# A hybrid decoder layer with a planned instruction order: expert rows ranked over all other steps, retention and the sample's logits as streams of their own

## The chip, the cores and the metric

The kernel runs on one core of one Trainium2 chip. The metric is device time in microseconds of one execution; the median of three runs before the change is 3858.67 us (3858.39 to 3861.91). The profile is of one further execution, which took 3870.04 us with a span of 3868.2 us from the first to the last instruction.

## The reference

One inference step of one decoder layer, for a prompt of 1024 tokens and a sample of 8 sequences with 4 new tokens each (32 tokens) over a paged cache of 2048 past tokens. All data are 32-bit floats.

```
xn  = rms_norm(x);  one projection of 1024 to 3400 columns gives q,k,v / indexer q,k,weights / retention q,k,v,gate
att = for every query: indexer score of every earlier key, keep the best 256, softmax attention over those (8 heads of 64)
ret = chunkwise retention (4 heads of 128, chunk 128, a state carried from chunk to chunk), group norm, swish gate
h   = x + concat(att, ret) @ w_out
n   = rms_norm(h);  8 heads: q = n @ w_q, two sets of 128 sub-keys, top 16 of each, top 16 of the 256 sums -> 128 experts per token
y   = h + sum over the 128 experts e of  gate_e * gelu(n . u[e]) * v[e]        # u, v: 16384 rows of 1024
out = rms_norm(y); also k, v, indexer k and the retention states
```

The expert part dominates the traffic: for each of 128 tokens of a tile and each of 128 expert slots the kernel reads one row of u and the row of v beside it (2048 floats, 8 KB).

## The kernel before

The 1024 prompt tokens are 8 tiles of 128 (t = 0 to 7); the 32 sample tokens are a ninth tile, SAMPLE (t = 8). First all nine tiles go through the input projection (step `project`), to about 470 us. Everything after that comes in one list of steps, `schedule`, which `make_schedule` (L342) writes before the kernel is built. Each engine walks that list and issues its own part of every step, so the list is the program order of each of the five in-order queues; semaphores alone hold the engines together. A step that waits holds up everything behind it on its engine.

Per tile there are three kinds of work.

- The front (`front_steps`, L226): load the projected rows into Hb, transpose q and k (`turn`), score all earlier keys (`score` on TensorE and ScalarE, `scored` on VectorE), the retention (`decay`, `decayed`, `hold`, `carry`, `carried`, `retained`), the search for the best 256 keys (`topk`: 32 rounds of MAX8 and MATCH_REPLACE8 on VectorE, L1345 and L1346), the mask, attention (`attend`, `soften`), `mixed`, and the transposes of the mix (`mixT`). The sample's front has its own steps: indexer keys gathered from the cache by sequence (`sscores`), retention with eight states (`sdecay`, `sret`, `skd`, `sstate`, `sstated`, `sstored`), its `topk` over 2080 keys on 32 partitions, then K and V gathered by sequence and attention in two groups of four sequences (`slogits`, `smask`, `sexp`, `sprobs`, `svalue`, `sout`). In the list the sample's `slogits` of sequences 0 to 3 stand between rounds of `topk`, in fixed places.
- The back (`back_steps`, L288): `out` (w_out in eight chunks, streamed in by SyncE), `norm`, queries, sub-key scores, the two levels of top 16 (`top`, `cand`, `best`), and `pick`, whose last instruction (L1467) says that the tile's experts are chosen.
- The expert stream: 128 rows per partition for a tile, 32 for the sample (where four partitions' worth of slots are packed). GpSimd gathers row after row (L1838, 128 x 8 KB each) into a ring of 8. Rows go in pairs (`unit`). VectorE multiplies and sums each u row with the normed tokens (the dot, L1484), ScalarE takes Gelu (L1755), VectorE multiplies by the gate (the coefficient, L1475), ScalarE writes a diagonal matrix of the coefficient (L1747), and TensorE adds diag x v into `yacc` (`sums`, L1030). Only then is the ring's slot free for the gather 8 rows later. `seed` (L1020) starts yacc with the residual, `ycopy` (L1763) copies it out, `finish` norms and stores it.

The coefficient of pair k-1 is no step: it stands inside `unit` k, behind the first of its two dots (L1485, `if k and s == PAIR * k: weigh_pair(t, k - 1)`); ScalarE's part of `unit` k writes the diagonals of pair k-1 first and then waits for pair k's dots. The last pair of a tile has a step `drain`.

The planner keeps two clocks, one for TensorE and one for VectorE, and takes at each turn the step that can start first; among those that can start within NEAR (0.4 us) of it, the one with the earliest due time. A front's steps are due evenly over PERIOD = 400 us from (t - 2) * PERIOD - 150 us, a back's over 360 us from (t - 1) * PERIOD, and dots and sums have due times as well:

```
yield "D", at, t * PERIOD + PERIOD * k / units(0), "unit"
yield "P", weighed[t, k] + 1.0, t * PERIOD + PERIOD * k / units(0), "sums"
```

So a front step that is due earlier than a pair comes before that pair. Fronts go one after another, so do backs; a back begins when its tile's front is done, the tile before is seeded and the tile two before is finished. `ycopy` follows the last sums of its tile in the list at once. It writes `ykeep`, which shares its place with nT, the next tile's transposed norm.

Of the kernel before, what the change touches and what calls it, by code (L numbers as in the profile page):

```python
# [226 lines left out]
def front_steps(t):  # L227
# [4 lines left out]
    if t < TILES:  # L232
# [10 lines left out]
        steps += [Step("decay", t, 0, "P", 1.2), Step("decayed", t, 0, "D", 2.3, 1, 0.3), Step("hold", t, 0, "P", 2.4, 1, 0.5),  # L243
                  Step("carry", t, 0, "P", 1.2, 0, 0.5), Step("carried", t, 0, "D", 1.4, 1, 0.3),
                  Step("retained", t, 0, "D", 2.3), Step("retained", t, 1, "D", 2.2), Step("retained", t, 2, "D", 2.6)]
# [9 lines left out]
    else:  # L255
        steps = [Step("load", t, 0, "", 0, 1, 12.0), Step("sheads", t, 0, "P", 3.0, 1, 2.5), Step("spad", t, 0, "D", 4.0, 2, 0.3),
                 Step("sdecay", t, 0, "P", 1.2, 2), Step("sdecayed", t, 0, "D", 4.5, 1, 0.3), Step("sret", t, 0, "P", 10.0, 1, 0.5)]
        for k in range(NB + 1):
            if k < NB:
                steps += [Step("skd", t, k, "D", 0.6, 0, 0.3), Step("sstate", t, k, "P", 1.7, 1, 0.4)]  # L260
            if k:
                steps += [Step("sstated", t, k - 1, "D", 1.4, 3 if k == 1 else 4 if k < NB else 2, 0.3)]
        steps += [Step("sstored", t, 0, "D", 0.2, 0, 0.3)]
        steps += [Step("retained", t, 0, "D", 2.3), Step("retained", t, 1, "D", 2.2), Step("retained", t, 2, "D", 2.6)]
        steps += [Step("sturn", t, 0, "P", 2.3), Step("sspread", t, 0, "D", 2.6, 1, 0.3), Step("swi", t, 0, "P", 2.8, 1, 0.4),
# [20 lines left out]
    return steps + [Step("mixT", t, 0, "P", 2.6, 1, 2.4)]  # L286


def back_steps(t):
# [15 lines left out]
    return steps  # L305

# [35 lines left out]
PERIOD, LEAD, ROW, LATENCY, NEAR = 400.0, 150.0, 2.62, 3.4, 0.4  # L342


def make_schedule():
# [11 lines left out]
    fronts = [Stream(front_steps(t), (t - 2) * PERIOD - LEAD, PERIOD) for t in range(TILES + 1)]  # L357
    backs = [Stream(back_steps(t), (t - 1) * PERIOD, 0.9 * PERIOD) for t in range(TILES + 1)]
    front = back = 0
    rows_at = 0.0  # L360
    chosen, keyed, mixed, seeded, finished, kept = {}, {}, {}, {}, {}, {}
    dotted, weighed, summed = {}, {}, {}
    dot, pair, drained = (0, 0), (0, 0), 0
# [9 lines left out]
    def heads():  # L373
        if front <= TILES:
            yield "front", fronts[front]
        if back <= TILES:
            yield "back", backs[back]

    def candidates():
        for kind, stream in heads():  # L380
            e = stream.head()
            what, t, _ = e.entry
            ready = stream.ready()
            names = (claimed + claims(*e.entry))[max(len(claimed) - 4, 0):]
            if any(freed_later(name) not in listed and freed_later(name) for name in names[:-4]):
                continue
            if what == "mixT" and t:
# [20 lines left out]
        if t in seeded and (t, k) in weighed:  # L408
            yield "P", weighed[t, k] + 1.0, t * PERIOD + PERIOD * k / units(0), "sums"
# [4 lines left out]
    while len(finished) <= TILES:  # L414
# [10 lines left out]
        if kind in ("front", "back"):  # L425
            stream = fronts[front] if kind == "front" else backs[back]
# [11 lines left out]
            if what == "mixT":  # L438
                mixed[t] = end
            if stream.head() is None and kind == "front":  # L440
                front += 1
            elif stream.head() is None:
                chosen[t] = end
                back += 1
        elif kind == "unit":
# [1495 lines left out]
```

## Time and profile before

| what | value |
|---|---|
| median of three runs | 3858.67 us |
| the profiled execution, its span | 3870.04 us, 3868.2 us |
| TensorE, VectorE, ScalarE, GpSimd busy | 82%, 69%, 26%, 32% of the span |
| TensorE's mean granted clock | 0.930 of full |
| read from and written to HBM | 1220.50 MB, 22.46 MB |
| gathers of expert rows | 1056 of 1.05 MB |

The stretches that count are read from tables of windows: busy time of each engine, the granted clock, the share of time in which the 16 DMA engines were busy, and the rate in GB/s. The rate is the one to watch in the expert stream, since each gather moves the same 1.05 MB.

### The profile page before, as it was taken

The numbers are of one execution on the slowest core, as the hardware profiler recorded it, in microseconds if no ns is written. First come the engines' busy times: TensorE is split into PE (matmuls) and PEld (weight loads), VectorE is DVE, ScalarE is ACT, GpSimd is POOL, SyncE is SP. The second block draws the span as 40 slices with busy tenths as digits, with TensorE's granted clock in tenths as the row PEclk, the third lists the DMA queues.
The fourth block names the chain that finished last, engine by engine and source line by source line (L and its number), as shares of the span: only waits on it lengthen the run. The fifth ranks groups of instructions, "written<-read, shape, count | busy, mean of one in ns | idle before, by whom it ended". The sixth has DMA issues, their size and how long they took to land.

```text
span 3868.2 us, 31404 instructions
## 1 busy us (share of the span) xinstructions
PE 3178.7 (82%) x9551; PEld 1543.8 (40%) x9551; DVE 2674.1 (69%) x6543; ACT 993.7 (26%) x2512; POOL 1237.8 (32%) x1084
## 2 busy tenths in 40 slices
PE   5999864988798879887987898689887389879776
PEld 2444253443354325433543453245433144334321
DVE  1222138888868778978888888988856998434655
ACT  1111122152134214421432153115222022311211
POOL 0000001444444434443443344234342124333443
PEclk9999977999999999998999899899999699889999
DMA  4111133999999999999999999889998179988998
GB/s 170 57 66 50 54 116 134 391 417 397 392 404 407 415 370 369 394 399 361 397 400 368 364 385 408 341 341 384 356 394 340 70 297 420 392 338 343 414 421 341
DMA packets 190425, 1245.72 MB, mean 322 GB/s; under 512 B 22704, under 2 KB 27184, under 8 KB 50672
## 3 DMA queue, kind: packets, MB, share of 16 engines
q0 software_dynamic: 155520, 1128.34, 72.4%
q1 hardware_dynamic: 34736, 115.37, 7.9%
q8 instruction: 77, 1.26, 0.1%
q14 instruction: 92, 0.75, 0.1%
HBM read 1220.50 MB, written 22.46 MB: 321 GB/s over the span
## 4 chain that ended last, share of the span: by engine, by line
PE 44%; DMA 26%; DVE 24%; issue 3%; ACT 1%; SPq 1%; POOL 1%; DVEq 0%; ACTq 0%; POOLq 0%
PE yacc L1030 23%; DMA weights<-in_uv,eid 19%; PE bank L857 11%; DVE weights L1484 7%; DVE kv L1346 3%; DVE tiny L1345 3%; PE bank L993 3%; DMA weights<-in_w_out 2%; PE bank L967 2%; DVE weights L1416 1%; DVE weights L1215 1%; DVE weights L1412 1%; DMA kv<-in_cache_ik,gi 1%; POOL weights L1838 1%; ACT diag L1747 1%
## 5 line engine op out<-in xcount | busy, mean ns | idle before, releaser
L1030 PE MATMUL yacc<-weights,diag 128*128 128x512 f32 (+1 forms) x4224 | 2002.5, 624 | 364.7 <-ACT diag L1747 363.4
L1838 POOL DMA_INDIRECT weights<-in_uv,eid x1056 | 1210.5, 1146 | 2578.1 <-PE yacc L1030 1875.8
L1484 DVE CUSTOM_DVE_ANT_0 weights<-weights,xn 128x1024 f32<-128x1024 f32 x1056 | 1290.2, 1224 | 597.5 <-DMA weights<-in_uv,eid 585.8
L1030 PEld LDWEIGHTS yacc<-weights,diag 128*128 128x128 f32 (+1 forms) x4224 | 802.5, 196 | 1453.6 <-issue 909.3
L1747 ACT ACTIVATE diag<-main,coef 128x128 f32<-128x128 f32 x1024 | 356.7, 394 | 1450.8 <-DVE coef L1475 1381.1
L1345 DVE MAX8 tiny<-kv 128x8 f32<-128x384 f32 (+6 forms) x224 | 245.0, 1094 | 3.0
L1755 ACT ACTIVATE gl<-hv 128x2 f32<-128x2 f32 x528 | 107.1, 203 | 530.6 <-DVE hv L1484 529.9
L1346 DVE MATCH_REPLACE8 kv<-tiny,kv 128x384 f32<-128x384 f32 (+6 forms) x224 | 241.6, 1079 | 0.0
L967 PE MATMUL bank<-weights 128*128 128x512 f32 (+1 forms) x288 | 158.4, 687 | 87.0 <-DMA weights<-in_w_out 85.8
L857 PE MATMUL bank<-weights 128*128 128x512 f32 (+3 forms) x560 | 229.6, 572 | 0.0
L857 PE MATMUL bank<-weights,mid 128*128 128x512 f32 (+1 forms) x448 | 183.2, 570 | 0.0
L857 PEld LDWEIGHTS bank<-weights 128*128 128x128 f32 (+1 forms) x560 | 97.4, 175 | 130.2 <-issue 125.4
L993 PEld LDWEIGHTS bank<-weights 128*128 128x128 f32 x1152 | 133.9, 192 | 16.0 <-issue 15.6
L1250 DVE TENSOR_TENSOR weights<-Hb,weights 128x80 f32<-128x80 f32 (+5 forms) x15 | 5.8, 387 | 190.6 <-ACT tinya L1637 190.3
L993 PE MATMUL bank<-weights 128*128 128x128 f32 (+1 forms) x1152 | 134.1, 275 | 0.8 <-ACT weights L1708 0.8
L967 PEld LDWEIGHTS bank<-weights 128*128 128x128 f32 (+1 forms) x288 | 56.7, 206 | 175.9 <-issue 173.9
L1416 DVE FIND_INDEX8 weights<-weights 128x8 uint32<-128x128 f32 (+1 forms) x396 | 125.4, 328 | 0.0
L857 PEld LDWEIGHTS bank<-weights,mid 128*128 128x128 f32 x448 | 84.8, 190 | 96.7 <-issue 91.8
L1412 DVE MAX8 weights<-weights 128x8 f32<-128x128 f32 (+1 forms) x396 | 112.6, 325 | 3.0 <-ACT weights L1732 1.6
L1250 DVE TENSOR_TENSOR weights<-spare,weights 128x80 f32<-128x80 f32 (+2 forms) x12 | 4.7, 389 | 142.2 <-ACT tinya L1637 141.9
L1475 DVE TENSOR_TENSOR coef<-gl,gate 128x2 f32<-128x2 f32 x528 | 82.3, 156 | 15.0 <-ACT gl L1755 14.6
L921 PEld LDWEIGHTS bank<-kv,mid 128*128 128x128 f32 x576 | 75.6, 198 | 35.0 <-issue 20.9
(240 smaller groups left out, 2309.8 us busy)
## 6 DMA issues: line engine op xcount, KB each, us to landing
weights<-in_w_out SPq DMA_DIRECT2D x72, 512.0 KB, 7.8
weights<-in_uv,eid POOLq DMA_INDIRECT x1056, 9.8
Hb<-h_scratch SPq DMA_DIRECT2D x8, 1700.0 KB, 10.7
weights<-in_w_in SPq DMA_DIRECT2D x6, 2048.0 KB, 18.8
h_scratch<-Hb SPq DMA_DIRECT2D x4, 1700.0 KB, 5.5
h_scratch<-spare SPq DMA_DIRECT2D x4, 1700.0 KB, 5.5
nw<-in_wffn SPq DMA_DIRECT2D x9, 512.0 KB, 6.4
nw<-in_wfin SPq DMA_DIRECT2D x9, 512.0 KB, 14.3
```

The lines of the kernel that those rows point to most:

```text
L857: mm = nc.tensor.matmul(b[0:R, 0:w], xT[t % 2][:, k, 0:R], win[:, k, 512 * n:512 * n + w], start=(k == 0), stop=(k == KC - 1))
L967: mm = nc.tensor.matmul(b[0:R, :], mixT[:, k, 0:R], wout_sb[i % 2][:, 512 * (k - k2):512 * (k - k2 + 1)], start=(k == 0), stop=(k == KC - 1))
L993: mm = nc.tensor.matmul(b[:, (h % 4) * R:(h % 4 + 1) * R], wq_sb[:, k, h * P:(h + 1) * P], nT[:, k, 0:R], start=(k == 0), stop=(k == KC - 1))
L1030: mm = nc.tensor.matmul(yacc[0:W, 512 * j:512 * (j + 1)], diag[:, n % 4, 0:W], ring[:, n % RING, D + 512 * j:D + 512 * (j + 1)], start=Fal ...
L1345: link(V.max(tiny[0:R, 40:48], a))
L1346: link(V.match_replace(a, tiny[0:R, 40:48], a, CHOSEN))
L1412: ins = V.max(vals[:, half], a)
L1416: ins = V.max_index(idxs[:, half], vals[:, half], a)
L1484: ins = V.tensor_tensor_reduce(u, u, xn[:, t % 2, :], 1.0, 0.0, ALU.mult, ALU.add, hv[:, n % RING:n % RING + 1])
L1747: A.activation(diag[:, n % 4, 0:W], select[:, 0:W], ACT.Copy, scale=coef[:, n % RING:n % RING + 1]).then_inc(diag_ready, 1)
L1755: A.activation(gl[:, c:c + PAIR], hv[:, c:c + PAIR], ACT.Gelu).then_inc(gelu_ready, 1)
L1838: pool.indirect_dma_start(dst, None, table, bass.IndirectOffsetOnAxis(ap=ids, axis=0)).then_inc(s, 16)
```

## The change

All of it but a few lines lies in the planner; no arithmetic is changed.

- `drain` is gone and the coefficient is a step `weigh` of its own on VectorE, with ScalarE's diagonals as its part there. It may start 0.75 us behind the pair's dots in the planner's clock.
- `unit`, `weigh` and `sums` have constant due times far below every other step's, so that among steps which can start within NEAR of the first they always come first. NEAR is 0.1 instead of 0.4.
- The retention of each tile leaves the front and becomes a stream (`side_steps`) that may begin when the tile's q and k are transposed. `attend` part 3, `mixT` and the sample's first `sscores` wait in the plan for its end; the sample's `sturn` waits for `sret`.
- The sample's `slogits` of sequences 0 to 3 leave the fixed places between `topk` rounds and become a stream (`past_steps`) that may begin when the sample's scores are in place; `smask` waits for its end. GpSimd's first K gather gets a wait for the sample's gated retention (`gated`). The sample's Silu moves from `retained` part 0 to part 1.
- `ycopy` becomes an entry of its own that waits in the plan for the next tile's `keys`.
- PERIOD is 360 instead of 400, LEAD 100 instead of 150; the sample's front is due 200 us later than the rule for the others gives, and over 0.8 of a period.

```diff
-PERIOD, LEAD, ROW, LATENCY, NEAR = 400.0, 150.0, 2.62, 3.4, 0.4
+PERIOD, LEAD, AHEAD, LATER, LAST, ROW, LATENCY, NEAR = 360.0, 100.0, 0.0, 200.0, 0.8, 2.62, 3.4, 0.1
@@ front_steps
-        steps += [Step("decay", t, 0, "P", 1.2), ... Step("retained", t, 2, "D", 2.6)]
@@ the sample's front
-        for k in range(ROUNDS):
-            steps += [Step("topk", t, k, "D", 4.8, 0, 0.3)]
-            if k % 8 in (1, 2, 3, 4, 5, 6):
-                steps += [Step("slogits", t, (k // 8, k % 8 - 1), "P", 2.0, 2)]
+        steps += [Step("topk", t, k, "D", 4.8, 0, 0.3) for k in range(ROUNDS)]
+def past_steps():
+    return [Step("slogits", SAMPLE, (b, c), "P", 2.0, 1, 1.2 if c < 5 else 4.0) for b in range(4) for c in range(6)]
@@ make_schedule
+    sides = [Stream(side_steps(t), (t - 2) * PERIOD - LEAD, 0.5 * PERIOD) for t in range(TILES + 1)]
+    pasts = [Stream(past_steps(), (SAMPLE - 2) * PERIOD + LATER, PERIOD)]
@@ candidates
+            if what == "mixT" or (what, part) in (("attend", 3), ("sscores", 0)):
+                if t not in held:
+                    continue
+                ready = max(ready, held[t])
-        if t in chosen and drained == t:
+        if due:
+            yield "D", dotted[due[0]] + 0.75, -2e7, "weigh"
+        if t in chosen:
-                yield "D", at, t * PERIOD + PERIOD * k / units(0), "unit"
-        if drained < t:
-            yield "D", dotted[drained, units(drained) - 1] + 0.8, -1e9, "drain"
+                yield "D", at, -1e7, "unit"
-            yield "P", weighed[t, k] + 1.0, t * PERIOD + PERIOD * k / units(0), "sums"
+            yield "P", weighed[t, k], -1e7, "sums"
+        if copying and (copying[0][0] == TILES or copying[0][0] + 1 in keyed):
+            yield "", copying[0][1], 0.0, "ycopy"
@@ VectorE
-                    if k and s == PAIR * k:
-                        weigh_pair(t, k - 1)
@@ ScalarE
-                if k:
-                    spread_pair(t, k - 1)
@@ GpSimd, slogits of sequence 0
+                    pool.wait_ge(gated, TILES + 1)
```

## Rows read from the trace of the kernel before

**Rows 1.** The page's first line.

```profile
span 3868.2 us, 31404 instructions
```

**Rows 2.** Windows of the expert streams (tiles 0-5, 6, 7, sample, quiet): stretch, length, busy (x), clock, DMA, GB/s.

```profile
650.00:2898.00 2248.00, 1920.50 (x5843) 953.39 (x5841) 1864.42 (x4578) 684.07 (x1677) 915.97 (x782) 0.94 0.96 385
2898.00:3417.00 519.00, 391.23 (x1268) 186.24 (x1264) 388.98 (x719) 122.23 (x307) 154.01 (x146) 0.88 0.77 308
3417.00:3778.00 361.00, 282.51 (x745) 122.07 (x744) 180.57 (x406) 62.71 (x204) 140.40 (x128) 0.93 0.95 382
3778.00:3868.20 90.20, 62.13 (x132) 13.98 (x130) 47.70 (x114) 12.65 (x49) 26.81 (x24) 0.93 0.82 336
3625.00:3775.00 150.00, 113.50 (x245) 44.47 (x244) 76.10 (x151) 26.91 (x90) 64.93 (x61) 0.99 1.01 421
```

**Rows 3.** Timeline of VectorE, the sample's key search: start, length, line, operation, tiles.

```profile
2964.68 2.32 DVE L1345 MAX8 tiny<-kv 32x8 f32<-32x2080 f32 x1
...
2967.11 2.30 DVE L1346 MATCH_REPLACE8 kv<-tiny,kv 32x2080 f32<-32x2080 f32 x1
...
3055.82 1.22 DVE L1484 CUSTOM_DVE_ANT_0 weights<-weights,xn 128x1024 f32<-128x1024 f32 x1
```

**Rows 4.** Timeline of TensorE there; in brackets the idle time before, and what ended it.

```profile
3057.62 6.43 PE L1030 MATMUL yacc<-weights,diag 128*128 128x512 f32 x8 [78.51 <-ACT diag L1747]
```

**Rows 5.** Waits in 650:2898 of TensorE, in 650:2732 of VectorE: total, times, longest.

```profile
PE bank L967 <- DMA weights<-in_w_out: 63.7, 12, 14.6
...
DVE weights L1484 <- DMA weights<-in_uv,eid: 246.7, 227, 9.5
```

**Rows 6.** Timeline of VectorE in the quiet stretch: two dots and a coefficient.

```profile
3644.71 1.23 DVE L1484 CUSTOM_DVE_ANT_0 weights<-weights,xn 128x1024 f32<-128x1024 f32 x1 [1.17 <-DMA weights<-in_uv,eid]
...
3647.19 1.23 DVE L1484 CUSTOM_DVE_ANT_0 weights<-weights,xn 128x1024 f32<-128x1024 f32 x1 [1.24 <-DMA weights<-in_uv,eid]
...
3648.34 0.16 DVE L1475 TENSOR_TENSOR coef<-gl,gate 128x2 f32<-128x2 f32 x1
```

**Rows 7.** Timeline of VectorE, retention of tile 0: first and last instruction.

```profile
488.05 0.69 DVE L1307 TENSOR_TENSOR spare<-bank,dec 128x512 f32<-128x512 f32 x1 [17.32 <-PE bank L879]
...
502.06 0.69 DVE L1301 TENSOR_TENSOR Hb<-Hb 128x512 f32<-128x512 f32 x1
```

**Rows 8.** Windows up to the end of the sample's search, and behind it (columns as Rows 2).

```profile
650.00:2732.00 2082.00, 1782.02 (x5368) 886.74 (x5366) 1758.07 (x4342) 644.82 (x1567) 846.58 (x726) 0.95 0.96 386
2732.00:2964.70 232.70, 200.97 (x663) 94.25 (x663) 136.94 (x308) 53.67 (x150) 89.60 (x75) 0.93 0.96 381
2964.70:3152.00 187.30, 92.02 (x344) 46.86 (x344) 184.41 (x177) 33.80 (x80) 32.13 (x32) 0.76 0.45 171
3152.00:3277.00 125.00, 113.05 (x365) 54.56 (x366) 105.69 (x323) 34.20 (x86) 48.13 (x45) 0.93 0.93 375
```

**Rows 9.** Window 2898:3152, the dots alone (two instructions each): VectorE, clock, DMA, GB/s.

```profile
2898.00:3152.00 254.00, 51.45 (x84) 0.83 0.60 232
```

**Rows 10.** Timelines: end of tile 7's front, end of search, sample's experts chosen, its seed.

```profile
2731.57 0.69 DVE L1382 TENSOR_TENSOR Hb<-bank,tiny 128x512 f32<-128x512 f32 x1
3151.99 1.23 DVE L1356 TENSOR_SCALAR kv<-kv 32x2080 f32<-32x2080 f32 x1
3612.93 0.19 DVE L1467 TENSOR_TENSOR gate<-gate,tiny 128x32 f32<-128x32 f32 x1
3777.68 1.95 PE L1020 MATMUL yacc<-h,main 32*128 32x512 f32 x4 [1.27 <-ACT weights L1764]
```

**Rows 11.** The page's DMA issues: KB, median us from issue to landing.

```profile
weights<-in_uv,eid POOLq DMA_INDIRECT x1056, 9.8
```

**Rows 12.** ScalarE: groups of loads ahead of Gelu (count, busy, mean ns), then timeline.

```profile
L1755 ACT ACT_TABLE_LOAD x65 | 83.4, 1283 | 1.2
...
2244.34 1.28 ACT L1755 ACT_TABLE_LOAD   x1
2245.64 0.20 ACT L1755 ACTIVATE gl<-hv 128x2 f32<-128x2 f32 x1
```

More of the change, by code:

```diff
@@ L256, in front_steps @@
         steps = [Step("load", t, 0, "", 0, 1, 12.0), Step("sheads", t, 0, "P", 3.0, 1, 2.5), Step("spad", t, 0, "D", 4.0, 2, 0.3),
[L257 to L260, printed above, removed]
-            if k:
[L262 to L265, printed above, removed]
+                 Step("sturn", t, 0, "P", 2.3, 1), Step("sspread", t, 0, "D", 2.6, 1, 0.3), Step("swi", t, 0, "P", 2.8, 1, 0.4),
                   Step("swiT", t, 0, "D", 1.6, 1, 0.3)]
@@ L356, in make_schedule @@
     clock = {"P": 0.0, "D": 0.0}
-    fronts = [Stream(front_steps(t), (t - 2) * PERIOD - LEAD, PERIOD) for t in range(TILES + 1)]
-    backs = [Stream(back_steps(t), (t - 1) * PERIOD, 0.9 * PERIOD) for t in range(TILES + 1)]
-    front = back = 0
+    fronts = [Stream(front_steps(t), (t - 2) * PERIOD - LEAD + (t == SAMPLE) * LATER, PERIOD if t < TILES else LAST * PERIOD)
+              for t in range(TILES + 1)]
+    backs = [Stream(back_steps(t), (t - 1) * PERIOD - AHEAD, 0.9 * PERIOD) for t in range(TILES + 1)]
+    sides = [Stream(side_steps(t), (t - 2) * PERIOD - LEAD, 0.5 * PERIOD) for t in range(TILES + 1)]
+    pasts = [Stream(past_steps(), (SAMPLE - 2) * PERIOD + LATER, PERIOD)]
+    front = side = back = past = 0
     rows_at = 0.0
     chosen, keyed, mixed, seeded, finished, kept = {}, {}, {}, {}, {}, {}
-    dotted, weighed, summed = {}, {}, {}
-    dot, pair, drained = (0, 0), (0, 0), 0
+    turned, held, returned, placed = {}, {}, [], []
+    dotted, weighed, summed, copying = {}, {}, {}, []
+    dot, due, pair = (0, 0), [], (0, 0)
     def arrival(t, k):
@@ L375, in heads @@
             yield "front", fronts[front]
+        if side <= TILES and side in turned:
+            yield "side", sides[side]
+        if not past and placed and SAMPLE in held:
+            yield "past", pasts[past]
         if back <= TILES:
@@ L381, in candidates @@
             e = stream.head()
-            what, t, _ = e.entry
+            what, t, part = e.entry
             ready = stream.ready()
@@ L386, in candidates @@
                 continue
+            if what in ("decay", "sdecay"):
+                ready = max(ready, turned[t])
+            if what == "mixT" or (what, part) in (("attend", 3), ("sscores", 0)):
+                if t not in held:
+                    continue
+                ready = max(ready, held[t])
+            if what == "sturn":
+                if not returned:
+                    continue
+                ready = max(ready, returned[0])
+            if what == "slogits" and part == (0, 0):
+                ready = max(ready, held[t], placed[0])
+            if what == "smask" and part == (0, 0):
+                if not past:
+                    continue
+                ready = max(ready, pasts[0].ends[-1])
             if what == "mixT" and t:
@@ L424, in make_schedule @@
             start = max(clock[on], start)
-        if kind in ("front", "back"):
-            stream = fronts[front] if kind == "front" else backs[back]
+        if kind in ("front", "side", "back", "past"):
+            stream = {"front": fronts[front:], "side": sides[side:], "back": backs[back:], "past": pasts}[kind][0]
             e = stream.head()
@@ L439, in make_schedule @@
                 mixed[t] = end
+            if (what, part) in (("turn", 3), ("spad", 0)):
+                turned[t] = end
+            if what == "sret":
+                returned.append(end)
+            if what == "splace":
+                placed.append(end)
+            if what == "retained" and part == 2:
+                held[t] = end
             if stream.head() is None and kind == "front":
                 front += 1
+            elif stream.head() is None and kind == "side":
+                side += 1
+            elif stream.head() is None and kind == "past":
+                past += 1
             elif stream.head() is None:
@@ L1755, in unit @@
                 A.activation(gl[:, c:c + PAIR], hv[:, c:c + PAIR], ACT.Gelu).then_inc(gelu_ready, 1)
-            def drain(t, part):
-                spread_pair(t, units(t) - 1)
             def ycopy(t, part):
```

51 lines of the change are left out of this document (30 added, 21 removed).

## The prediction

> **What bounds the kernel now.** I read the windows of the expert streams first. In the quiet stretch nothing but pairs of rows is left, and there the DMA engines are busy all the time at 421 GB/s [rows 2]. A row is 1.05 MB, so a row every 2.49 us is the ceiling, and time below it can be counted as lost: length times (1 - rate/421). Tiles 0 to 5 lose 2248 x (1 - 385/421) = 192 us, tile 6 loses 519 x (1 - 308/421) = 139 us, tile 7 loses 361 x (1 - 382/421) = 33 us. That is 364 us out of 3128. VectorE and TensorE are not far behind the DMA: in 650 to 2732 they are busy 84% and 86% [rows 8]. So three resources are nearly full, and the order decides how well they overlap.
>
> Next I read where tile 6 loses its time. VectorE starts the sample's search at 2964.68 and takes the next dot at 3055.82; between them lie 19 rounds of 4.76 us (a MAX8 of 2.32, a replace of 2.30, a short load) and one small addition [rows 3]. TensorE stands 78.5 us, waiting for a diagonal [rows 4]. The rows in the ring had long landed: the plan had put the search, due earlier, in front of the dots. The window of the search runs at 171 GB/s and loses 187.3 x (1 - 171/421) = 111 us by itself [rows 8].
>
> Last I read what the end hangs on. The sample's experts are chosen at 3612.9, its seed comes only at 3777.7, when tile 7 is done [rows 10]. The sample was 165 us early, the stream was late. Then 90.2 us follow to the end [rows 2].
>
> **The change part by part.** No instruction goes except the coefficient's place; the arithmetic is the same, so everything is a matter of waits.
>
> *Dots and sums first.* The search stall goes. A round of search can now stand before a pair only if the pair was not there when the round began, 4.76 us at most, against 8 rows x 2.49 = 19.9 us in the ring. The gain is at least the 78.5 us of TensorE's wait and at most all 139 us that tile 6 loses. Tile 7, which has no search beside it, still loses 33 us, so I take 100.
>
> *The coefficient as its own step.* In the quiet stretch a pair's second dot ends at 3645.94 and its coefficient starts at 3648.34, behind the next pair's first dot [rows 6]: 2.4 us, of which Gelu needs 0.20 [rows 12]. So about 2.2 us of a slot's 19.9 come back. Where the DMA runs at the ceiling that is worth nothing; where slots run out it is worth up to that. This and the rank work on the same 192 us of tiles 0 to 5. Of these, 63.7 us of TensorE waiting for chunks of w_out [rows 5] are not touched: SyncE still issues `finish`, `resid` and the w_out loads in that order. Between nothing and 192 - 64 = 128 us can come back; VectorE and TensorE, both over 84% busy, have no room for all. I take half, 64 us, a third of the 192.
>
> *Retention as a stream.* On tile 0 the retention stands on VectorE from 488.05 to 502.75 ahead of the mask, and VectorE had been idle 17.3 us before it [rows 7]. Run beside attention it saves 0 to 14.7 us ahead of the first chosen tile; I take 7. For the later tiles it is work for VectorE's gaps and counted below. What is late in its place is attention itself, which shares TensorE's banks.
>
> *Logits, gather wait, ycopy.* The 24 sample logits ran between search rounds and now run beside them. An estimate of one step per pair in the quiet stretch, 24 x 2 x 2.49 = 120 us, is covered by the search's 32 x 4.76 = 152 us, so `smask` waits for the search as before: nothing. The wait on GpSimd has row gathers queued behind it, so every microsecond of it would stop the stream; it ends with the retention, which the plan puts before the scores: nothing. `ycopy` behind the next tile's keys costs nothing as long as those are early, and the sample's experts were 165 us early [rows 10]; with that cover gone, seed and all sums of the next tile wait behind it on TensorE.
>
> *The sum for the streams.* 100 + 64 + 7 = 171 us. Tile 7 ends at 3778 - 171 = 3607.
>
> *The price: the sample comes later.* Dots before the search means the search ends later, and the sample was not far enough ahead for the whole of it. Up to the end of the search at 3152 VectorE idles (2082 - 1758) + (232.7 - 136.9) + (187.3 - 184.4) = 423 us [rows 8, 10]. By then tile 6 had 84/2 = 42 dots [rows 9]. In the new order tile 6 is nearly through when the search ends, some 120 dots: 78 more at 51.45/42 = 1.23 us and half a coefficient of 0.16 [rows 6], 1.31 us together: 102 us. Tile 7's back has to be done by then too; before, VectorE did most of it in 3152 to 3277, where it was busy 105.7 us, of which 125 us x 375 GB/s = 45 rows account for 59 us [rows 8]: 47 us more. Against this stands idle time won back. In 650 to 2732 VectorE waits 246.7 us for rows in 227 places [rows 5], with other work in the list behind the wait; with the coefficient free and the retention as filler I take a third of the 324 us, as for the streams: 108 us. Bounds are nothing and the 247 us. The search then ends at 3152 + 102 + 47 - 108 - 7 = 3186. From there to the sample's experts it took 3613 - 3152 = 461 us, through logits, V gathers, w_out and the back, on engines shared with a stream as now: chosen at 3647. That is 40 us after tile 7 has ended. The first row lands 9.8 us later [rows 11], then 90.2 us: 3747.
>
> The span falls from 3868.2 [rows 1] by 121 us. The profiled execution took 3870.04 us, 11.4 above the median of the runs, so against the median: 3858.7 - 121, about 3740.
>
> **The rivals.**
>
> *The streams set the end* (0.20). If VectorE wins back more than 160 us of its 423, the sample is chosen before tile 7 ends, and the end is 3607 + 90 = 3697, against the median 3688, down to 3640 if the streams win back all that w_out leaves. For it: 0.96 of the DMA's time is busy in 650 to 2898 already [rows 2], so little is missing. Against it: VectorE's load in the late tiles.
>
> *The plan's clocks don't hold* (0.17). The order is fixed before the run; if the planned arrivals miss, VectorE still stands before a dot with other work behind it, as in those 227 places. Then only the search stall and the 7 us go (85 us), VectorE wins nothing back, fewer rows are done by then (some 100: 76 us), and the search ends at 3152 + 76 + 47 - 7 = 3268: chosen at 3729, end at 3829, against the median 3820.
>
> *Slower: VectorE waits in the coefficient, and the sample's search is pushed past the end of the streams* (0.18). The coefficient now follows its own dots and not the next pair's first dot, so the time Gelu needs is no longer covered. Gelu is often late: 65 times a table load of 1.28 us stands before it [rows 12], usually because an Exp of the attention came between. If nothing is planned in that gap, VectorE, with all front and back steps queued behind, stands up to 65 x 1.28 = 83 us. For it: those loads lie in the attention, where VectorE has no slack. Against it: the plan puts the coefficient 0.75 us behind the dots and takes any other ready step in between. With nothing won back and 83 us lost the search ends at 3294 + 83 = 3377, the experts are chosen at 3838; the last stretch then runs without a stream beside it, which I put at 45 us shorter, and the end is 3893, against the median about 3880. It decides from a loss of about 13 us: with 13 us more idle than before the search ends at 3307, and 3307 + 461 + 100 is the old end.
> The Trainium skill (ScalarE: Activation LUTs, What ACT_TABLE_LOAD costs) states about 1.28 us for the load and 1.38 us of drain, 2.66 us for every switch. By that the 65 loads would make 173 us and this rival some 90 us worse. The trace agrees with the load and shows no drain behind it: the load at 2244.34 ends at 2245.62 and Gelu starts at 2245.64 [rows 12], so the sum goes by 1.28.
>
> **How the numbers follow.** My forecast has 0.45, its own range is 3690 to 3800. The range over all cases is 3640 to 3880: below lies the best of the first rival, above half of the slower one. 0.2%, some 8 us, is about what a measurement of this kernel can tell from no change. Forecast, first and second rival make 0.82; of the second's upper edge 0.04 falls within 0.2%, and of the slower one's lower edge 0.03. So faster 0.78, the same 0.07, slower 0.15.
>
> **What would show it.** Right: no search round stands in front of landed rows for more than two rounds, and TensorE's longest wait for a diagonal is under 20 us; in the quiet stretch the coefficient starts within 1 us of its dots; the window from the first to the last tile reaches over 395 GB/s in tiles 0 to 5; the sample's experts are chosen after tile 7's last sums, and the DMA rate has a hole of some 50 us between. The waits for w_out stay near 64 us. Wrong: coefficients that wait for Gelu more than 60 us in total; a search that ends before 3100 or after 3300; a tile other than the sample whose experts come after the tile before has ended; a gather on GpSimd that waits for the retention.

## The result, and the profile after

The changed kernel takes 3920.53 us (median; 3914.46 to 3922.50) against 3860.29 for the one before on the same chip: a ratio of 1.0153 [1.0135, 1.0170], 1.5% slower. The forecast of 3740 us was wrong in sign and outside its range. The profiled execution has a span of 3920.6 us, 52.4 longer than [rows 1].

First the page: the span, and the rate in 40 slices of 98 us. Two slices stand out: the 34th (3234 to 3332) with 11 GB/s and the 39th (3725 to 3823) with 95.

```profile
span 3920.6 us, 31491 instructions
...
GB/s 168 67 61 42 80 88 184 394 411 411 378 400 400 421 367 394 414 380 366 420 414 373 381 410 412 420 399 405 289 265 411 410 366 11 249 421 405 385 95 345
```

The kernel before has one such slice, the 32nd with 70 GB/s, which lies in its search; its page:

```profile
GB/s 170 57 66 50 54 116 134 391 417 397 392 404 407 415 370 369 394 399 361 397 400 368 364 385 408 341 341 384 356 394 340 70 297 420 392 338 343 414 421 341
```

Next the windows, with the columns of [rows 2]: up to the end of tile 7's front, up to the start of the sample's search, the search, up to the choice of the sample's experts, and the rest. The sixth is the first empty stretch, the part of the search that runs alone; the last is the second.

```profile
650.00:2805.30 2155.30, 1857.59 (x5564) 921.66 (x5564) 1831.68 (x4477) 658.39 (x1646) 882.24 (x767) 0.96 0.97 395
2805.30:3164.00 358.70, 283.30 (x945) 141.45 (x945) 216.47 (x607) 74.21 (x209) 127.81 (x119) 0.89 0.90 364
3164.00:3349.00 185.00, 74.66 (x198) 29.78 (x198) 179.01 (x155) 30.95 (x76) 25.35 (x23) 0.72 0.35 139
3349.00:3818.00 469.00, 369.89 (x1142) 180.17 (x1142) 214.47 (x468) 95.13 (x260) 152.40 (x139) 0.88 0.79 323
3818.00:3920.00 102.00, 60.80 (x128) 13.20 (x128) 52.22 (x118) 12.84 (x50) 32.93 (x32) 0.90 0.84 341
3237.00:3341.00 104.00, 14.20 (x51) 5.45 (x50) 102.53 (x67) 11.30 (x21) 0.94 (x1) 0.58 0.03 10
3775.00:3817.00 42.00, 29.01 (x129) 24.89 (x128) 14.55 (x62) 4.92 (x8) 0.00 (x0) 0.50 0.00 2
```

The first row answers to the first of [rows 8]: up to the end of tile 7's front the rate rose from 386 to 395 GB/s, but that front ended 74 us later (2805 against 2732). VectorE's idle time there is 2155.3 - 1831.7 = 324 us; before it was 2082 - 1758 = 324 us. Up to that point of the work not a microsecond came back.

The waits of the whole execution say where rows stopped (total, times, longest). GpSimd's wait for a choice of experts contains 647.3 us ahead of tile 0, which the kernel before has too; what is left is 240.4 us in three places, and before there was none.

```profile
POOL weights L1875 <- DVE gate L1514: 887.7, 4, 647.3
DVE weights L1531 <- DMA weights<-in_uv,eid: 484.8, 407, 10.4
...
PE yacc L1077 <- ACT diag L1789: 282.6, 194, 22.3
...
PE bank L1014 <- DMA weights<-in_w_out: 120.3, 17, 31.4
...
PE bank L1210 <- DVE kv L1403: 98.1, 1, 98.1
DVE coef L1522 <- ACT gl L1795: 91.0, 122, 14.4
```

The timelines show the three places. First GpSimd, with the idle time in brackets: the gather that starts tile 6, tile 7 and the sample each waits for its choice.

```profile
2812.34 0.94 POOL L1875 DMA_INDIRECT weights<-in_uv,eid  x1 [30.98 <-DVE gate L1514]
...
3369.44 0.94 POOL L1875 DMA_INDIRECT weights<-in_uv,eid  x1 [125.29 <-DVE gate L1514]
...
3818.07 0.94 POOL L1875 DMA_INDIRECT weights<-in_uv,eid  x1 [84.14 <-DVE gate L1514]
```

Then ScalarE, copying out tile 6:

```profile
3242.54 0.60 ACT L1800 ACTIVATE weights<-yacc 128x512 f32<-128x512 f32 x1 [2.65 <-PE yacc L1077]
```

Tile 6 ended at 3243, 165 us earlier than before (3408), and tile 7's experts were not yet chosen. TensorE:

```profile
3350.10 7.21 PE L1210 MATMUL bank<-kv,dec 32*128 32x512 f32 x8 [98.15 <-DVE kv L1403]
```

It stands 98 us in the sample's masked attention (`smask`), waiting for the end of the search. VectorE shows why both wait:

```profile
3232.22 2.31 DVE L1392 MAX8 tiny<-kv 32x8 f32<-32x2080 f32 x1
...
3339.40 2.30 DVE L1393 MATCH_REPLACE8 kv<-tiny,kv 32x2080 f32<-32x2080 f32 x1
3341.73 2.29 DVE L1262 TENSOR_TENSOR weights<-weights,main 128x2048 f32<-128x2048 f32 x1
...
3348.82 1.23 DVE L1403 TENSOR_SCALAR kv<-kv 32x2080 f32<-32x2080 f32 x1
...
3368.88 0.29 DVE L1514 TENSOR_TENSOR gate<-gate,tiny 128x128 f32<-128x128 f32 x1
...
3817.61 0.19 DVE L1514 TENSOR_TENSOR gate<-gate,tiny 128x32 f32<-128x32 f32 x1
```

From 3237 to 3342 stand 22 search rounds without a break (MAX8 and replace, 2.3 us each), behind the last coefficient of tile 6; only then come the last steps of tile 7's choice (the TENSOR_TENSOR of 3341.73 is the first), done at 3368.88. The sample is chosen at 3817.61.

VectorE again, a coefficient in the quiet stretch:

```profile
3639.94 0.08 DVE L1531 DVE_READ_ACCUMULATOR2_ANT hv<- 128x1 f32 x1
3640.29 0.18 DVE L1522 TENSOR_TENSOR coef<-gl,gate 128x2 f32<-128x2 f32 x1 [0.27 <-ACT gl L1795]
```

It follows its dot by 0.3 us, where it stood 2.4 us behind [rows 6].

The table orders the events (us of the span; a tile is done with its last sums; "busy, idle" is VectorE's from 650 to the search's end, "rowless" GpSimd's wait for choices after tile 0's). Tile 7's copy out is no measure of its end: it now waits in the plan for the sample's keys and comes 49 us behind the last sums in the changed kernel.

| kernel | tile 6 done | tile 7 chosen | search ends | sample chosen | tile 7 done | VectorE busy, idle | rowless | ratio to before |
|---|---|---|---|---|---|---|---|---|
| before | 3408 | 3277 | 3152 | 3613 | 3776 | 2079, 423 | 0 | 1 |
| after | 3243 | 3369 | 3349 | 3818 | 3753 | 2227, 472 | 240 | 1.0153 |
| coefficient alone | 3377 | 3293 | 3144 | 3639 | 3755 | 2083, 411 | 0 | 0.9961 |
| rank alone | 3256 | 3422 | 3361 | 3816 | 3809 | 2187, 524 | 143 | 1.0151 |
| streams alone | 3372 | 3317 | 3281 | 3737 | 3786 | 2187, 444 | 0 | 1.0038 |
| all but the rank | 3337 | 3298 | 3261 | 3728 | 3762 | 2198, 413 | 0 | 0.9979 |
| all but the coefficient | 3231 | 3336 | 3316 | 3777 | 3721 | 2216, 450 | 202 | 1.0046 |
| search due 100 us later | 3234 | 3134 | 3517 | 3751 | 3583 | 2372, 495 | 132 | 0.9971 |
| rank in the search only | 3226 | 3104 | 3425 | 3725 | 3586 | 2334, 441 | 101 | 0.9908 |

### The profile page after: what moved, and what is told of

It reads as the page before. It is cut to its first block, busy times and chain, and to the rows that moved or that the text cites. A ratio compares the mean times of both kernels' runs of the same rounds, so it can differ in the third digit from the quotient of the medians.

```text
span 3920.6 us, 31491 instructions
## 1 busy us (share of the span) xinstructions
PE 3170.2 (81%) x9551; PEld 1555.6 (40%) x9551; DVE 2684.7 (68%) x6543; ACT 982.2 (25%) x2513; POOL 1222.9 (31%) x1084
## 4 chain that ended last, share of the span: by engine, by line
PE 49%; DMA 26%; DVE 17%; issue 3%; ACT 2%; POOL 2%; SPq 1%; ACTq 0%; DVEq 0%; POOLq 0%
PE yacc L1077 26%; DMA weights<-in_uv,eid 19%; PE bank L904 10%; DVE weights L1531 4%; PE bank L1040 4%; DVE kv L1393 3%; DVE tiny L1392 3%; PE bank L1014 2%; DMA weights<-in_w_out 2%; POOL weights L1875 2%; DMA out_y_p<-nw 1%; ACT diag L1789 1%; DVE weights L1262 1%; DVE weights L1463 1%; PE bank L953 1%
## 5 line engine op out<-in xcount | busy, mean ns | idle before, releaser
L1077 PE MATMUL yacc<-weights,diag 128*128 128x512 f32 (+1 forms) x4224 | 1969.9, 616 | 284.0 <-ACT diag L1789 282.6
L1875 POOL DMA_INDIRECT weights<-in_uv,eid x1056 | 1196.5, 1133 | 2630.2 <-PE yacc L1077 1681.5
L1531 DVE CUSTOM_DVE_ANT_0 weights<-weights,xn 128x1024 f32<-128x1024 f32 x1056 | 1273.0, 1223 | 491.8 <-DMA weights<-in_uv,eid 484.8
L1077 PEld LDWEIGHTS yacc<-weights,diag 128*128 128x128 f32 (+1 forms) x4224 | 792.8, 194 | 1362.3 <-issue 896.2
L1014 PE MATMUL bank<-weights 128*128 128x512 f32 (+1 forms) x288 | 156.0, 680 | 122.8 <-DMA weights<-in_w_out 120.3
L1040 PE MATMUL bank<-weights 128*128 128x128 f32 (+1 forms) x1152 | 156.9, 301 | 10.0 <-ACT weights L1750 10.0
L1040 PEld LDWEIGHTS bank<-weights 128*128 128x128 f32 x1152 | 155.4, 219 | 21.9 <-issue 12.7
L1210 PE MATMUL bank<-kv,dec 32*128 32x512 f32 x16 | 14.6, 1052 | 98.1 <-DVE kv L1403 98.1
```

The source lines that it names most:

```text
L1014: mm = nc.tensor.matmul(b[0:R, :], mixT[:, k, 0:R], wout_sb[i % 2][:, 512 * (k - k2):512 * (k - k2 + 1)], start=(k == 0), stop=(k == KC - 1))
L1040: mm = nc.tensor.matmul(b[:, (h % 4) * R:(h % 4 + 1) * R], wq_sb[:, k, h * P:(h + 1) * P], nT[:, k, 0:R], start=(k == 0), stop=(k == KC - 1))
L1077: mm = nc.tensor.matmul(yacc[0:W, 512 * j:512 * (j + 1)], diag[:, n % 4, 0:W], ring[:, n % RING, D + 512 * j:D + 512 * (j + 1)], start=Fal ...
L1531: ins = V.tensor_tensor_reduce(u, u, xn[:, t % 2, :], 1.0, 0.0, ALU.mult, ALU.add, hv[:, n % RING:n % RING + 1])
L1875: pool.indirect_dma_start(dst, None, table, bass.IndirectOffsetOnAxis(ap=ids, axis=0)).then_inc(s, 16)
```

## The experiments

Three theories stood at the start. R: the rank puts rows ahead of the sample's search, the sample becomes late, and the end is the search's end + 469 + 103 us. W: the waits for Gelu in the new coefficient step take VectorE's time. H: the 125 us hole ahead of tile 7 is the loss. After the first four kernels a fourth was formed, P: what chooses experts (fronts and backs) and what uses them (rows) share VectorE; ranking the rows first brings rows earlier and the choices later, until rows wait for a choice. The edits are excerpts; a line of `...` stands for lines left out. The experiments ran on three chips, each beside the kernel before, and the ratios are to that; a difference in us between two kernels is of their medians.

**The coefficient step alone**, put on the kernel before.

```diff
+        if due:
+            yield "D", dotted[due[0]] + 0.75, -2e7, "weigh"
...
-                    if k and s == PAIR * k:
-                        weigh_pair(t, k - 1)
```

> The kernel before with one part of the change: the coefficient is a step of its own; ranks, streams and constants are as before. Theory R (the rank of dots and sums over all other steps makes tile 7's front and the sample's search late, and the end is the search's end + 469 + 103 us): without the rank the early coefficient only helps, time 3760 to 3840, search end at 3152 or earlier. Theory W (VectorE now waits for Gelu in front of the coefficient, 91 us against 15, and that is the loss): slower than before, about 3935. Theory H (the 125 us in which nothing is gathered, since tile 7's last back steps stand behind 21 search rounds, is the loss): says nothing of this run; it would follow the place of tile 7's back.

Median 3850.27, ratio 0.9961 [0.9945, 0.9976]: faster, though 10 us above what R had expected, with nearly the waits of after. From the list of waits:

```profile
DVE weights L1482 <- DMA weights<-in_uv,eid: 468.2, 387, 5.6
...
DVE coef L1473 <- ACT gl L1746: 88.1, 141, 14.3
```

88.1 us of waiting for Gelu and a faster kernel: W falls. VectorE waits 468.2 us for rows, where before it was 585.8 in the whole execution, and 14.6 for Gelu: 600 us of both before, 556 here. Most of what it no longer waits ahead of a dot it waits ahead of a coefficient.

**All but the coefficient step**: the changed kernel with the coefficient back inside `unit`.

```diff
-        if due:
-            yield "D", dotted[due[0]] + 0.75, -2e7, "weigh"
-        if t in chosen:
+        if t in chosen and drained == t:
...
```

> The changed kernel with the coefficient put back behind the next pair's first dot (and the drain step); rank, streams and constants as changed. Theory W: VectorE's waits for Gelu fall from 91 to about 15 us and the time to about 3845. Theory R: the rank is still there, the search ends as late or later, 3350 to 3410, time 3920 to 3980. Theory H: the hole stays, time within 20 us of 3920.

3882.28, ratio 1.0046 [1.0018, 1.0075]: still slower than before, and 38 us under the changed kernel. No theory had this time: W expected 3845, H at least 3900, R at least 3920.

From its waits, in the order GpSimd, TensorE, VectorE:

```profile
POOL weights L1887 <- DVE gate L1516: 848.5, 3, 646.5
...
PE bank L1212 <- DVE kv L1405: 81.0, 1, 81.0
...
DVE coef L1524 <- ACT gl L1804: 7.1, 5, 5.2
```

The waits for Gelu are gone (7.1 us), the holes (848.5 - 646.5 = 202 us) and TensorE's stand in `smask` (81 us) are not. So the pattern belongs to the rank, and under the rank the coefficient step adds to it.

**All but the rank**: due times for dots and sums again.

```diff
-                yield "D", at, -1e7, "unit"
+                yield "D", at, t * PERIOD + PERIOD * k / units(0), "unit"
...
-            yield "P", weighed[t, k], -1e7, "sums"
+            yield "P", weighed[t, k], t * PERIOD + PERIOD * k / units(0), "sums"
```

> The changed kernel with dots and sums ranked by due time as before; coefficient step, streams and constants as changed. Theory R: tile 7's front is done before 2760 instead of 2805, the search ends 60 to 100 us earlier (3250 to 3290), time 3780 to 3860. Theory W: the coefficient step is still there, time 3900 to 3940. Theory H: if the hole stays at 100 us or more, time 3900 or more; a shorter time with the hole still there would speak against it.

3853.62, ratio 0.9979 [0.9964, 0.9994]. Taking the rank out gives 67 us back.

From its waits:

```profile
POOL weights L1875 <- DVE gate L1514: 646.9, 1, 646.9
...
DVE coef L1522 <- ACT gl L1795: 98.9, 125, 15.1
```

No hole is left (646.9 us is tile 0's), and there are more waits for Gelu than in after, 98.9 us. That is what R expected, and once more against W; for H it decides nothing, since the hole went with the rank.

**The search due 100 us later**, rank kept.

```diff
-PERIOD, LEAD, AHEAD, LATER, LAST, ... = 360.0, 100.0, 0.0, 200.0, 0.8, ...
+PERIOD, LEAD, AHEAD, LATER, LAST, ... = 360.0, 100.0, 0.0, 300.0, 0.8, ...
```

> The changed kernel with one constant: the sample's front is due 300 us late instead of 200, so that in the list all of tile 7's back stands ahead of the sample's search. Theory H: the hole of 125 us before tile 7 goes, time about 3795. Theory R: the search is pushed further behind, ends at about 3450 to 3530, and the time rises to 3990 or more although tile 7's rows flow without a hole; a hole of 200 us or more stands before the sample's rows instead. Theory W: no difference, 3900 to 3940.

3856.83, ratio 0.9971 [0.9953, 0.9990]. Now tile 7's last back steps come before the search and it is chosen at 3134, ahead of tile 6's end.

Windows of its search and of the stretch from there to the sample's choice:

```profile
3234.00:3517.00 283.00, 224.69 (x505) 89.70 (x503) 276.48 (x372) 62.00 (x189) 114.08 (x105) 0.94 0.98 393
3517.00:3751.00 234.00, 182.72 (x733) 103.81 (x732) 57.64 (x175) 48.18 (x105) 34.01 (x32) 0.81 0.45 167
```

and GpSimd's wait for choices, tile 0's 646.6 us included:

```profile
POOL weights L1875 <- DVE gate L1514: 778.6, 3, 646.6
```

The search stretches from 3234 to 3517, but beside rows: VectorE is busy 276.5 of 283 us and the rate is 393 GB/s, where the search of after had 139. So a late search does no harm here, where rows flow beside it. And from the search to the choice there are only 234 us, at 167 GB/s: the 469 of R is no constant. That the chain is longer when it runs beside a fuller stream is my reading. R holds as a description of after, not as a rule. H had the place right and the size wrong: without the hole the loss is gone, but the gain stays under the hole's 125 us, since 101 us of GpSimd's waiting now stand ahead of the sample.

**The rank alone**, put on the kernel before.

```diff
-                yield "D", at, t * PERIOD + PERIOD * k / units(0), "unit"
+                yield "D", at, -1e7, "unit"
...
-            yield "P", weighed[t, k] + 1.0, t * PERIOD + PERIOD * k / units(0), "sums"
+            yield "P", weighed[t, k] + 1.0, -1e7, "sums"
```

> The kernel before with one part of the change: dots and sums come first among the steps that can start; the coefficient stays behind the next pair's first dot, and streams and constants are as before. Theory P (fronts and backs, which choose the experts, share VectorE and TensorE with the dots and sums; a rank over them makes rows earlier and choices later, and the rows then wait for a choice): tiles end earlier than before up to tile 5, the choices of tiles 6 to 8 come 20 us or more later than before (2783, 3277, 3613), GpSimd waits for a choice in holes of 100 us or more in total behind the first tile, time 3890 to 3930. Theory W (the coefficient step's waits for Gelu are the loss): no such waits here, time 3860 or less.

3922.44, ratio 1.0151 [1.0130, 1.0171]: the whole loss from two lines (NEAR stays 0.4 here).

The list of waits (GpSimd's with 652.9 us of tile 0), then a window:

```profile
POOL weights L1838 <- DVE gate L1467: 795.8, 5, 652.9
...
PE bank L1163 <- DVE kv L1356: 87.9, 1, 87.9
...
DVE coef L1475 <- ACT gl L1755: 7.0, 6, 4.5
```

```profile
3200.00:3500.00 300.00, 153.13 (x512) 71.93 (x511) 252.49 (x440) 58.72 (x135) 55.34 (x53) 0.76 0.47 185
```

The same two marks as in after: 795.8 - 652.9 = 143 us without a choice, 87.9 us of TensorE behind the search, and 185 GB/s in 3200 to 3500. VectorE waits 7.0 us for Gelu here, so the loss needs no such waits and W falls for good. P is borne out: tile 5 ends 77 us earlier than before, and the choices of tile 6, tile 7 and the sample come 65, 145 and 203 us later.

**The rank only while the sample's search is under way**, with the search due 100 us later.

```diff
-PERIOD, LEAD, AHEAD, LATER, LAST, ... = 360.0, 100.0, 0.0, 200.0, 0.8, ...
+PERIOD, LEAD, AHEAD, LATER, LAST, ... = 360.0, 100.0, 0.0, 300.0, 0.8, ...
@@ due time of "unit" and of "sums"
-    -1e7
+    -1e7 if front == TILES and fronts[front].head() and fronts[front].head().entry[0] == "topk" else t * PERIOD + PERIOD * k / units(0)
```

> The changed kernel, but dots and sums rank over the others only while the sample's search is the next step of the fronts; elsewhere they go by due time as before. The sample's front is due 300 us late instead of 200, so that tile 7's back stands ahead of the search. Theory P: the choices up to tile 6 come as with the old rank (tile 6 at about 2750), tile 7's before tile 6's rows end, so no hole there; the search runs beside rows at 380 GB/s or more and ends at about 3430 to 3480; time 3780 to 3820, faster than both kernels. If instead the stretch from the search's end to the sample's choice has a fixed length (467 us, theory R in its first form), the time is 4000 or more. Theory W: the waits for Gelu stay near 60 to 90 us, time as with LATER = 300 alone, about 3857.

3829.83, ratio 0.9908 [0.9886, 0.9930]: faster than both kernels, though 10 us above what was expected. The later search with no rank at all was not run, so how much of this gain is the rank's is open.

Its windows, and GpSimd's wait (649.8 us of it ahead of tile 0):

```profile
650.00:2800.00 2150.00, 1860.60 (x5645) 931.60 (x5644) 1832.08 (x4485) 660.25 (x1638) 872.06 (x760) 0.94 0.97 392
2800.00:3200.00 400.00, 331.43 (x986) 152.52 (x985) 284.28 (x676) 92.42 (x264) 172.63 (x146) 0.94 0.98 396
3200.00:3500.00 300.00, 246.48 (x608) 104.75 (x608) 254.64 (x373) 63.21 (x190) 129.10 (x113) 0.93 0.97 388
3500.00:3830.00 330.00, 227.72 (x745) 105.57 (x745) 115.12 (x293) 55.27 (x151) 64.38 (x62) 0.82 0.59 232
```

```profile
POOL weights L1875 <- DVE gate L1514: 750.8, 2, 649.8
```

In the three windows up to 3500 the rate is 388 GB/s or more. Then comes the price that is left: 750.8 - 649.8 = 101 us in which the sample's rows wait for its choice.

**The streams and constants alone**: the changed kernel with due times and the coefficient in `unit` (the edits of the second and third kernel above together).

```diff
-        if due:
-            yield "D", dotted[due[0]] + 0.75, -2e7, "weigh"
...
-                yield "D", at, -1e7, "unit"
+                yield "D", at, t * PERIOD + PERIOD * k / units(0), "unit"
...
```

> The changed kernel without rank and without the coefficient step: retention, the sample's first logits and ycopy as streams, and the new constants, are left. Theory P: choices and tile ends within some 30 us of before, the search's stall of rows is back (TensorE's longest wait for a diagonal 50 us or more), time 3850 to 3880. If the streams were what delays the sample (its scores wait for the end of its retention), the search would end at 3250 or later and the time would be 3900 or more with the old rank as well.

3877.79, ratio 1.0038 [1.0021, 1.0055]: retention and logits as streams, with the new periods, bring nothing by themselves and cost 0.4%. The time is as P expected, but not the order: the search ends at 3281 and the sample is chosen at 3737, 129 and 124 us later than before, where P had some 30. So most of the 197 us by which the search ends later in after come without the rank. They cost little here because the sample is still chosen 48 us before tile 7's last sums. TensorE's longest stand before a diagonal is only 36.6 us (P had 50 or more), so half of the search stall goes without the rank too (the search is due later here, which I take to be the reason).

**Half of the search left out** of the changed kernel.

```diff
-        steps += [Step("topk", t, k, "D", 4.8, 0, 0.3) for k in range(ROUNDS)]
+        steps += [Step("topk", t, k, "D", 4.8, 0, 0.3) for k in range(ROUNDS // 2)]
```

> The changed kernel with 16 of the sample's 32 search rounds left out (the sample then keeps 128 keys, not 256), 76 us of VectorE's work; all else as changed. Theory P: tile 7's last back steps and the sample's chain stand behind those rounds, so the hole of 125 us before tile 7 shrinks to about 50, tile 7's choice comes near 3290, the sample's near 3740, and the time falls by about 76 us to 3835 to 3855. If the end hung on the rows (the gathers' rate over all) and not on the choices, the time would stay within 20 us of 3920, as no row is left out.

3828.71, ratio 0.9906 [0.9872, 0.9941]: 92 us less than after for 16 x 4.76 = 76 us of VectorE, and 6 us under the range that P gave. Search end, sample's choice and the end each come 79, 93 and 92 us earlier. No row was left out, so the rows' rate alone does not set the end. In after, work of the search is paid in full: it stands on the path to the end.

**The coefficient planned later**, 2.0 us behind its dots instead of 0.75.

```diff
-            yield "D", dotted[due[0]] + 0.75, -2e7, "weigh"
+            yield "D", dotted[due[0]] + 2.0, -2e7, "weigh"
```

> The changed kernel with one number in the plan: the coefficient may start 2.0 us behind its dots instead of 0.75, so that other steps are put between. Theory W (VectorE standing in the coefficient step, waiting for Gelu, is what the step costs under the rank): the waits fall from 91 to under 45 us and the time by about 40 us to some 3880. Theory P: the waits fall too, but the choices of tiles 7 and 8 still stand where the plan puts them, time 3900 to 3925.

3907.10, ratio 1.0109 [1.0076, 1.0142].

From its waits (647.0 us of the first ahead of tile 0):

```profile
POOL weights L1875 <- DVE gate L1514: 858.0, 3, 647.0
...
DVE coef L1522 <- ACT gl L1795: 74.9, 121, 13.9
```

The waits for Gelu fall by 16 us only and the holes to 211 us. The time lies in the range of P and not at the 3880 of W, but the step is too small to settle anything.

**The best order without the coefficient step.**

```diff
-        if due:
-            yield "D", dotted[due[0]] + 0.75, -2e7, "weigh"
-        if t in chosen:
+        if t in chosen and drained == t:
...
```

> The fastest kernel so far (rank only beside the sample's search, sample 300 us late) with the coefficient put back behind the next pair's first dot. Theory P: with the old rank in tiles 0 to 6 the early coefficient is worth some 25 us, as between the run of the streams alone (3878) and that with old rank and coefficient step (3854), so 3845 to 3865 here. Theory W: without the step's waits (55 us in that kernel) the time is 3800 or less.

3849.58, ratio 0.9981 [0.9947, 1.0015], as P expected. The coefficient step is worth 20 us in the best order (28 by the ratios, as the two kernels ran on different chips), 24 without the rank (3878 to 3854) and some 15 (0.39%) on the kernel before; only under the full rank does it cost (38 us).

## Why the prediction was wrong

The failed step is "I take a third of the 324 us" of VectorE's idle time, 108 us won back. The rows showed that VectorE waited for rows; they did not show that a step behind such a wait was ready to run. Nothing was won back; the search's end shows it, term by term. Predicted was 3152 + 102 + 47 - 108 - 7 = 3186. VectorE's mask at the end of the search starts at 3348.8, 197 us later than in [rows 10].

- Busy time up to there: predicted 102 + 47 = 149 us more, measured 2227.2 - 2079.4 = 148. The dots that were pulled ahead of the search (128 of tile 6 against 46: 82 more, 78 assumed), and tile 7's back, cost what the rows said. That the rank pulls them was right only in part: with the streams and constants alone 56 of the 82 were ahead of the search.
- Idle time: predicted 108 us less, measured 49 more (472 against 423). That is 157 of the 174 us by which the span was missed.
- Search to choice: 461 assumed, 469 measured. Choice to end: 100 assumed, 103 measured. The 7 us of the retention: tile 0 chosen 2 us earlier.

What the idle time did can be read from VectorE's waits up to the search's end, here of after in 650 to 3349:

```profile
DVE weights L1531 <- DMA weights<-in_uv,eid: 297.2, 266, 10.4
DVE h L1438 <- PE bank L1014: 52.7, 5, 24.5
DVE coef L1522 <- ACT gl L1795: 49.6, 47, 9.9
```

The same three before, in 650 to 3152:

```profile
DVE weights L1484 <- DMA weights<-in_uv,eid: 332.1, 277, 9.5
DVE h L1391 <- PE bank L967: 24.1, 5, 12.8
DVE coef L1475 <- ACT gl L1755: 7.6, 5, 2.7
```

Waiting for rows fell by 35 us (the coefficient free, as argued); waiting for Gelu in the coefficient rose by 42, and waiting for w_out's product ahead of an addition of the back by 29. That is 36 of the 49 us. The wait moved from ahead of the dot to behind it. In every kernel of the study VectorE idles 316 to 357 us between 650 and 2800, before 338: no order of this study won that third. I read it so: a VectorE that serves each row as soon as it lands waits for the next, wherever in its list the wait stands.

With no time won, what goes to rows is taken from the choices. The second failed assumption stood in the same paragraph: that tile 7's back is done by the search's end at the cost of 47 us. The top-16 search of that back was done by then, its last steps were not: tile 7 was chosen at 3369, behind the search, where I had it chosen before tile 6 was through. Before, the experts were chosen 74 us (tile 2) to 164 us (sample) ahead of the end of the tile in front. After, the lead is 65, 59, 71, 54 and 25 us for tiles 1 to 5, then -11, -126 and -65. The lead is the buffer between what chooses and what uses. With the rank alone it is 76, 74, 65, 20, -20, -31, -167 and -6: the rank spent it, and where it is below zero the streams stop. With the coefficient alone it is 33 to 116 us, and no row waits for a choice after tile 0's. The end of the changed kernel hangs on the sample's choice: tile 7's last sums are through 65 us before it.

What was right. The search stall is gone: TensorE's longest wait for a diagonal is 22.3 us, against 78.5 [rows 4] and the 20 named. In the changed kernel that shows little, since 22 of the 32 rounds came behind tile 6's last row; but in the kernel with the later search, where rows flow beside the whole search, it is 22.4. The streams gained what was forecast as long as they were fed: tile 6 ended 165 us earlier, where 100 + 64 + 7 = 171 was the sum to tile 7's end. That the sum fits so well is luck: by the end of tile 5 there were 93 us, where 64 + 7 were forecast, and tile 6 added 72, with a hole of 31 us ahead of it, where 100 were. The coefficient follows its dots at once. The rate in tiles 0 to 5 is 395 GB/s. The waits for w_out, which were to stay near 64 us, are 75.9 there, 120.3 in all. The sample is chosen 65 us after tile 7's last sums (40 forecast), with a hole of 84 us in the gathers ahead of it (some 50 forecast). Of the signs named as wrong three appeared: over 60 us of waits for Gelu, a search that ends after 3300, and experts chosen after the tile before had ended. The gather on GpSimd did not wait for the retention.

The rivals. "The streams set the end" needed 160 us of idle time won back. "The plan's clocks don't hold" came nearer with its idle term (nothing won back; measured 49 us more), but counted 76 us for rows ahead of the search and none for the waits that rise: it gave 3820. The slower rival named the outcome, the search pushed past the streams' end, with 3377 and 3838 for the search's end and the choice (3349 and 3818 measured). The last stretch, which it made 45 us shorter, was not: 469 and 103 us. The loss does not need its cause: waits for Gelu grew by 42 us up to the search's end, but the rank alone loses as much with 7.0 us of them, and the coefficient step alone has 88.1 and is faster. Under the full rank the step does cost 38 us. The point at which it decides, 13 us more idle than before, was stated rightly: with 49 more the end lay beyond the old one. By the Trainium skill (ScalarE: Activation LUTs, What ACT_TABLE_LOAD costs), with 2.66 us for every switch, its 65 loads would have made 173 us. The trace does not bear that out: no drain shows behind the load [rows 12], and VectorE's waits for Gelu came to 91.0 us in all.

What is shown and what stays open. Shown: the rank by itself makes the loss (1.0151 alone; 67 us back when it is taken out of the whole), and the order of the search against tile 7's back makes the hole (100 us later, and the hole is gone). The effect is not additive: with streams and constants but without the coefficient step the rank costs only 4 us (3878 to 3882), since tile 7's last sums come 65 us earlier there while the sample's choice comes 40 us later: without the rank tile 7 sets the end, with it the sample's choice. Open: why the coefficient step helps by 15 to 28 us in three orders and costs 38 under the full rank. Its pairs come through earlier (tile 5's end, 2801 against 2840) and the search ends 33 us later, which fits P, but it was not isolated.

## What to carry to other kernels

Before ranking a stream over the work that feeds it, read the lead: how long before it is needed each batch of feed is ready. If the shared engine is as busy as VectorE here (84%), count no idle time as won unless an experiment shows it; then every microsecond given to the stream comes out of the lead, and when that is gone the stream stops. Rank the stream first only in the stretch where the feed has time to spare, and order feed against feed by who is needed first: the fastest kernel here did both, in and ahead of the one long search, though the two were not taken apart.

## What had not been expected of the hardware

In both empty stretches TensorE's granted clock falls to about half: 0.50 in 3775 to 3817, which is 1.2 GHz instead of 2.4, with TensorE busy 29.0 of 42 us, and 0.58 in 3237 to 3341 with 14.2 of 104. In both the sums of rows had stopped before, at 3753 and by 3243. The end of the sample's chain, which has to close the second stretch, so runs at the lower clock. What that costs can be read from the sample's queries, first after, then before, where rows flow beside them and the clock is 1.00:

```profile
3770.61 13.87 PE L1040 MATMUL bank<-weights 128*128 128x32 f32 x64 [0.37 <-ACT weights L1750]
...
3566.97 3.65 PE L993 MATMUL bank<-weights 128*128 128x32 f32 x32
```

The 128 matmuls take 27.7 us after and 14.6 before, so the lower clock costs 13 us in this step.

The search on VectorE and a full row stream can share the chip: in the kernel with the later search VectorE is busy 276.5 of 283 us at 393 GB/s. The search itself then takes 283 us, where it took 187 before.
